# Feed-forward products of a two-layer encoder step: PSUM banks and product order in the up and down tiles

## What is computed

```python
def _convffn(h, buf, w_up, conv_w, w_down):
    a = jnp.einsum('bld,df->blf', h, w_up)           # 1024 -> 5632
    a, buf_new = _causal_dwconv(a, buf, conv_w)      # depthwise, width 3
    gate, up = jnp.split(a, 2, axis=-1)
    return jnp.einsum('blf,fd->bld', jax.nn.silu(gate) * up, w_down), buf_new
...
x = x + _convffn(_rmsnorm(x, norm2_g), ...)
```

## Time and profile before

| What | Before |
|---|---|
| Median of 3 runs | 3636.01 us |
| Profiled execution | 3637.06 us |
| Its span | 3635.3 us |
| Mean granted TensorE clock | 0.954 |
| PE busy | 3325.8 us (91%), 23900 matmuls |
| PE weight loads | 3075.7 us (85%), 23900 |
| DVE / ACT / POOL busy | 2013.1 (55%) / 908.0 (25%) / 885.6 (24%) us |

### The profile page before, as it was taken

One profiled execution on the slowest core, in us unless ns is written; L12 is line 12 of the kernel. 1 busy time (PEld: TensorE's weight loads), 2 busy tenths in 40 slices (PEclk: granted clock), 3 DMA queues, 4 the chain that ended last, 5 costly groups with the idle time before them and its releaser, 6 DMA issues. The chain is left out here.

```text
span 3635.3 us, 57209 instructions
## 1 busy us (share of the span) xinstructions
PE 3325.8 (91%) x23900; PEld 3075.7 (85%) x23900; DVE 2013.1 (55%) x3500; ACT 908.0 (25%) x1662; POOL 885.6 (24%) x780
## 2 busy tenths in 40 slices
PE   5988989798999999999988889987899999999996
PEld 4866876587999999999987678756889999999996
DVE  7466435474455566555655644445645556556556
ACT  3244124333211111111233322342332111111111
POOL 2221120112322222222332201201133222222222
PEclk9999999798999999999989999987999999999998
DMA  6621222201111111111163212312011111111112
GB/s 208 183 78 61 84 73 91 72 9 39 39 44 39 46 41 41 35 47 41 34 192 120 78 56 73 112 40 79 13 39 39 41 42 46 35 47 41 41 41 74
DMA packets 121076, 232.70 MB, mean 64 GB/s; under 512 B 33892, under 2 KB 82788, under 8 KB 117416
## 3 DMA queue, kind: packets, MB, share of 16 engines
q1 hardware_dynamic: 120808, 228.93, 19.4%
HBM read 174.34 MB, written 54.18 MB: 63 GB/s over the span
## 5 line engine op out<-in xcount | busy, mean ns | idle before, releaser
L260 PE MATMUL PS<-h_split,w_split 128*128 128x384 f32 x3072 | 1068.4, 348 | 28.2 <-PEq L198 16.1
L262 PE MATMUL PS<-h_split,w_split 128*128 128x384 f32 x3072 | 1045.2, 340 | 0.0
L261 PE MATMUL PS<-h_split,w_split 128*128 128x384 f32 x3072 | 1041.8, 339 | 0.0
L255 POOL TENSOR_TENSOR w_split<-w_full,w_split 128x1024 fp32r<-128x1024 f32 x194 | 472.1, 2434 | 1047.3 <-ACT w_split L247 1047.3
L260 PEld LDWEIGHTS PS<-h_split,w_split 128*128 128x128 f32 x3072 | 587.2, 191 | 50.4 <-issue 36.7
L261 PEld LDWEIGHTS PS<-h_split,w_split 128*128 128x128 f32 x3072 | 583.8, 190 | 2.3 <-issue 0.6
L262 PEld LDWEIGHTS PS<-h_split,w_split 128*128 128x128 f32 x3072 | 583.8, 190 | 0.0
L247 ACT CAST w_split<-w_full 128x1024 fp32r<-128x1024 f32 x194 | 201.8, 1051 | 1320.5 <-PE PS L262 1181.7
L2279 DVE TENSOR_TENSOR x<-x,PS 128x384 f32<-128x384 f32 x528 | 285.7, 553 | 178.2 <-PE PS L262 176.5
L260 PE MATMUL PS<-ffn_act,w_split 128*128 128x384 f32 x1056 | 367.4, 348 | 8.2 <-POOL w_split L255 7.1
L261 PE MATMUL PS<-ffn_act,w_split 128*128 128x384 f32 x1056 | 357.0, 338 | 0.0
(11 more groups left out here) (385 smaller groups left out, 4889.3 us busy)
## 6 DMA issues: line engine op xcount, KB each, us to landing
w_full<-in_w_up SPq DMA_DIRECT2D x88, 512.0 KB, 3.3
w_full<-in_w_down SPq DMA_DIRECT2D x44, 512.0 KB, 3.3
w_full<-in_w_in SPq DMA_DIRECT2D x38, 512.0 KB, 3.4
kq_keep<-split_rows SPq DMA_DIRECT2D x128, 128.0 KB, 2.4
kq_row<-kq_keep SPq DMA_DIRECT2D x32, 512.0 KB, 4.3
x<-x_keep SPq DMA_DIRECT2D x2, 4608.0 KB, 14.8
w_full<-in_w_out SPq DMA_DIRECT2D x16, 512.0 KB, 3.2
gdn_y<-y_keep SPq DMA_DIRECT2D x2, 3456.0 KB, 12.8
```

Of the source, the lines that this page charges most:

```text
L255: pool.tensor_tensor(ws[:, n % SSLOTS, 1, 0:w], wf[:, n % WSLOTS, 0:w], ws[:, n % SSLOTS, 0, 0:w].bitcast(F32), ALU.subtract).then_inc(w_l ...
L260: pe.matmul(out, w_hi, a_hi, start=first, stop=False)
L261: pe.matmul(out, w_hi, a_lo, start=False, stop=False)
L262: return pe.matmul(out, w_lo, a_hi, start=False, stop=last)
```

## The change

For up tiles with c of 2 or more, the three token blocks go on side by side in three banks (0 to 2 for even c, 3 to 5 for odd c): the loops are k, part, block, so that each matmul is in another bank than the one before it. Before such a tile PE waits once, until DVE has taken the whole tile c - 2. Tiles 0 and 1 keep their order and use the new banks; block 2 of tile 1 waits for the square roots, as bank 5 holds a square sum until then. Down units alternate between banks 6 and 7, so that unit u waits until unit u - 2 has been added. The numbers of matmuls, weight loads and DVE instructions stay.

```diff
+                sum_bank = (6, 7, 5)
+
+                def up_bank(c, b):
+                    return PS[:, 3 * (c % 2) + b, 0:BLK]
...
+                            if c >= 2:
+                                pe.wait_ge(upf, (c - 1) * NB)
+                                for k in range(KD):
+                                    for part, side in ((0, 0), (0, 1), (1, 0)):
+                                        for b in range(NB):
+                                            mm = pe.matmul(up_bank(c, b), ws[:, slot, part, k * P:(k + 1) * P],
+                                                           h2[:, side, k, b * BLK:(b + 1) * BLK],
+                                                           start=(k == 0 and part == 0 and side == 0),
+                                                           stop=(k == KD - 1 and part == 1))
+                                            if k == KD - 1 and part == 1:
+                                                mm.then_inc(upr, 1)
+                                continue
                             for b in range(NB):
-                                u = c * NB + b
-                                if u >= 4:
-                                    pe.wait_ge(upf, u - 3)
+                                if c == 1 and b == 2:
+                                    pe.wait_ge(rtd, NB)
...
-                                    mm = split_product(pe, PS[:, u % 4, 0:BLK], ws[:, slot, 0, k * P:(k + 1) * P],
+                                    mm = split_product(pe, up_bank(c, b), ws[:, slot, 0, k * P:(k + 1) * P],
...
-                                    pe.matmul(PS[:, 4 + b, 0:BLK], ones[:, :], ss[:, b, :], start=True,
+                                    pe.matmul(PS[:, sum_bank[b], 0:BLK], ones[:, :], ss[:, b, :], start=True,
...
-                                if u >= 4:
-                                    pe.wait_ge(added, u - 3)
+                                if u >= 2:
+                                    pe.wait_ge(added, u - 1)
...
-                                    mm = split_product(pe, PS[:, 4 + u % 4, 0:BLK], ws[:, slot, 0, m * P:(m + 1) * P],
+                                    mm = split_product(pe, PS[:, 6 + u % 2, 0:BLK], ws[:, slot, 0, m * P:(m + 1) * P],
...
-                            src = PS[:, u % 4, 0:BLK]
+                            src = up_bank(c, b)
...
-                        dve.tensor_tensor(xs, xs, PS[:, 4 + u % 4, 0:BLK], ALU.add).then_inc(added, 1)
+                        dve.tensor_tensor(xs, xs, PS[:, 6 + u % 2, 0:BLK], ALU.add).then_inc(added, 1)
```

More of the change, by code:

```diff
@@ L2163, in _ @@
                         act.wait_ge(rcd, b + 1)
-                        act.sqrt(ss[:, b, :], PS[:, 4 + b, 0:BLK]).then_inc(rtd, 1)
+                        act.sqrt(ss[:, b, :], PS[:, sum_bank[b], 0:BLK]).then_inc(rtd, 1)
                     for n, (kind, c, t) in enumerate(tiles):
@@ L2213, in invert @@
                         dve.wait_ge(smr, b + 1)
-                        s = PS[:, 4 + b, 0:BLK]
+                        s = PS[:, sum_bank[b], 0:BLK]
                         link(dve.tensor_scalar(s, s, 1.0 / D_MODEL, EPS, ALU.mult, ALU.add))
```

## The result

The changed kernel took 3699.48 us in the median of 4 runs (3687.03 to 3700.05) against 3634.62 of the kernel before (4 runs); the ratio is 1.0168, with a 95% interval from 1.0144 to 1.0192. The forecast was 3695. Its profiled execution took 3699.4 us, with a span of 3697.5.

What follows compares the result with a forecast made beforehand. PE was taken as the bound, busy 91% of the span. Down-pair losses of 48.6 + 6.6 + 3.6 = 58.8 us on 3637.06 gave 3695.9, less 1.1 for the profiled execution: 3695 us, range 3660 to 3732.

Steps and rivals of the forecast that it cites:

- Up order: Up tiles, 6048 matmuls now changing bank each time: 0 gain, with 3 ns a matmul (18 us) either way not excluded.
- the full-price rival: Up matmuls: change of bank removes 15.5 ns each, 94 us in all, giving about 3601 us; chance 0.09.
- Waits of up and the square sums: Up tiles: waits for the earlier tile, for bank 5 in tile 1 and for weight slots cost 0.
- All blocks finish together: End of an up tile: DVE's takes and the work behind them come 0.60 us later, uncovered at a down pair.
- Two down banks: Ordinary down pairs: units wait for adds, 3.4 us lost, net 2.7 us x 18 pairs = 48.6 us.
- Tenth and last pair: Those down pairs in both layers: extra waits for adds, net 6.6 us for the tenth and 3.6 for the last.
- The steady-state rival: Down pairs behind unit 6: 0.07 us slack is missed, every second unit restarts, 28 us more, 3723; chance 0.13.
- The clock rival: Down pairs: new PE idle times bring half clock, 10 to 30 us more, 3705 to 3725; chance 0.13.
- the main case: Whole kernel: the forecast itself, 58.8 us lost on PE's path, mostly in down waits, 3695 us; chance 0.55.
- The forecast's own range: Whole kernel: 3680 to 3712 us, from 3 ns a matmul down or half of it up.
- the 58.8: All down pairs: summed loss in us, 48.6 + 6.6 + 3.6, all on PE's path.

Runs made afterwards that it cites:

- the two runs above: Kernel before, up units of tiles 2 on in order part, then k: 3627.55 us; changed kernel, up tile's two inner loops swapped: 3680.67 us.
- the staggered run: Changed kernel with the last of an up tile's eight k steps done block by block, so blocks end one after another: 3685.45 us, ratio 1.0128.
- The runs with late pieces: Changed kernel, a down pair's first three adds without convolution pieces: 3638.79 us; first four without, then pieces at every second add: 3622.57 us.

## Why the prediction was right

Point by point:

- **Up order, taken as 0 with 3 ns either way.** The bank has no part in it, as the unit ends in the earlier trace rows had said, and the full-price rival is refuted by the two runs above. But the term was mis-sized: the new order of operands gave 1.4 ns a matmul, 8.5 us over 6048, of which 7.5 lie between the down pairs. The prediction had looked at equal weights side by side, not at the moving operand. The formula that it took from the Trainium skill (TensorE: Matmul & The Clock Gate, Back-to-back issue gap) is there for an isolated matmul, so 175.5 ns in a stream with a load for each matmul doesn't contradict it.
- **Waits of up and the square sums, 0.** Right: past tile 0 no up load of the changed kernel waits.
- **All blocks finish together, 0.60 us.** Right in kind and nearly in size; the staggered run takes 0.5 us back from each pair.
- **Two down banks, net 2.7 us x 18 = 48.6.** The 12 pairs without a fall of the clock took 28.35 to 28.59 us, 28.49 on average, against 25.85 before: 2.64 each, 47.5 us over 18. The five ends of adds hit to 0.05 us. A unit was taken as 1.05 us, where a pair without waits is 24.97 (1.04 a unit), so the losses before and after were each put 0.2 us low, which drops out of the difference. The instruction of 2.53 us ends 0.62 behind L255 (1213.89 and 1213.27), not with it. What the step didn't part is its cause. It named the alternation of add and piece, and had the 2.53 us instruction beside it as a number. The runs with late pieces give the shares of 28.58 - 24.97 = 3.6 us: 2.3 are the shift and the piece that meets L255, 0.8 the alternation at 1.21 us, and 0.4 is left with late, spaced pieces, which four banks save (an ordinary pair is 25.40 and 24.97 us there).
- **Tenth and last pair, 10.2 us.** They and what lies between them took 15.5. The waits come where they were put, at units 7 and 10 of the tenth pair and unit 16 of the last, which starts 2.2 us late for the forecast 2.4. What the forecast lacked is the clock: from the tenth pair's start on each layer has 13.7 us at half clock, where it had 3.4. The staggered run and the one with three banks and the old order have these same waits with 3.4 us at half clock, and there the two pairs cost 8.1 us over both layers. Their tenth pair is free of the shift too, about 0.5 us each, so some 6 of the 15.5 are the clock's, an estimate from these runs.
- **The steady-state rival** (0.07 us of slack). Refuted: behind unit 6 no load waits in any ordinary pair.
- **The clock rival.** It came, beside the main case and not in its place: six pairs of 18, 0.6 to 1.3 us each above the mean of the others, 5.8 us, and the 6 at the layers' ends. The prediction had it at 10 to 30 us.
- **The forecast's own range**, 3680 to 3712: the terms that it names give 3677 and 3704. Nothing else hangs on these bounds.

So the mechanism was right, and how close the sum came is in part luck: the 58.8 stands against 61.3 because two terms left out, -7.5 for the operands and +12 for the clock, partly cancel.

## What to carry over

Halving the banks of a consumer cuts the lag that it may have by more than half: count it in time (banks less one, times the unit; here three units of 1.05 us became one) against the longest run of other work between two of its evacuations, at the worst overlap. Before taking banks for a rearrangement, check in the old trace whether a change of bank alters the distance of two matmuls; here it didn't, and the order could be had without it. Work that is cut into pieces between evacuations is best put where no other engine's instruction can stretch a piece. With no bank moved, that and the turned up order together gave the fastest version: against the kernel before, its ordinary pairs took 15.8 us less and the up tiles between them 7.3. Late pieces with the old up order weren't run.

## What was not expected of the hardware

- The distance of fp32r matmuls of 384 columns depends on the sequence of their operands, by up to 2 ns: 175.5 and 174.1 ns in the up tiles, 173.5 and 175.5 in the down units, and in the up tiles it is the same in one bank and in three.
- A DVE instruction on SBUF alone that met POOL's subtraction ended only 0.63 us behind it, after 2.96 us in place of 0.83, even one with a single tensor input; adds with one input in PSUM kept 539 to 557 ns beside it. It goes the other way too: POOL's copy L2151 takes 0.20 us by itself and 0.74 where DVE's scale, begun just before, is running, and L255 starts later by as much. POOL's and DVE's timelines of the changed kernel:

```profile
1224.06 0.74 POOL L2151 COPY ffn_new<-ffn_row 128x16 f32<-128x16 f32 x1
1224.76 2.36 POOL L255 TENSOR_TENSOR w_split<-w_full,w_split 128x1024 fp32r<-128x1024 f32 x1
```
```profile
1223.91 0.83 DVE L2261 TENSOR_SCALAR ffn_gate<-ffn_row,par 128x1168 f32<-128x1168 f32 x1
```

- The clock halves behind idle times shorter than the 3.55 us of the earlier trace rows: one of 2.08 us brought a fall in one pair and none in the next, with the same rows ahead of it. It cost 1.4 us there, where no other long wait followed, and 0.6 to 1.3 us in the changed kernel's pairs, where PE waits anyway. And the 3.55 us don't always bring one: in the run with one bank and the new order, the window behind them in the first layer stays at 1.00, and that layer's tenth and last pairs took 57.6 us where the second layer's, with a fall, took 59.0. PE's timeline of that run, and a window of 4 us from there:

```profile
1793.30 0.44 PE L260 MATMUL PS<-ffn_act,w_split 128*128 128x384 f32 x1 [3.55 <-POOL w_split L255]
```
```profile
1793.30:1797.30 4.00, 4.00 (x23) 4.00 (x24) 1.66 (x3) 1.05 (x2) 0.42 (x1) 1.00 0.68 155
```

- The wait alone doesn't settle whether a fall comes. With the same delays of 0.24 and 1.74 us, the 18 ordinary pairs had none in the run with two down banks alone and none with three banks and the old order, but eight in the staggered run. With the idle time of 2.08 us it was every second pair, nine of 18. What decides is open.
